# Trunk inference step on one core: cumulated gates spread by transposes of a repeated column, the fox bias added by VectorE, the decays masked ahead of the fox maxima

## The chip, the cores and the metric

The kernel runs as one program on 1 core of a Trainium2 chip. The metric is device time in microseconds (us), median of several runs; a smaller number is better. TensorE is called PE here, VectorE DVE, ScalarE ACT, GpSimd POOL, and the engine that issues all transfers SP.

## The reference, cut to what matters

Two decoder layers run over a prompt of 256 tokens and over 8 sampled tokens, each of which has 1024 past tokens. In each layer a half-step FFN is followed by four groups of heads that one projection feeds, and by a second half-step FFN. Three of the groups matter here: B, forgetting ("fox") attention, whose logits get the cumulated log gates; C, the gated delta rule; A, windowed attention with a partial rotation ("rope"). The same groups attend for the 8 sampled tokens over a paged cache.

```python
def fox_attend(q, k, v, cum_k, cum_q, q_pos):
    s = einsum('nqhd,nkhd->nhqk', q, k) * HEAD_DIM ** -0.5
    s = s + cum_q[..., :, None] - cum_k[..., None, :]
    s = where(k_pos[None, :] <= q_pos[:, None], s, -inf)
    return einsum('nhqk,nkhd->nqhd', softmax(s), v)
...
# group C, in chunks
gcum = cumsum(gch, axis=-1)
decay = exp(where(i[:, None] >= i[None, :], gcum[..., :, None] - gcum[..., None, :], -inf))
a_mat = where(strict, einsum('...id,...jd->...ij', kbeta, kc) * decay, 0.0)
t_mat = triangular_solve(eye + a_mat, eye)
```

## The kernel before, in words

Each engine has its own program, written out by hand in the order in which it runs, and waits on named semaphores. There is no scheduler. Each layer is a row of stages: gate and up products, down products, the input projection, then the mixing stage ("mix", from PE's transposes at L1714 to the output projection), the output projection and the second FFN. The dense stages run fp32 as three products of rounded parts. The change touches only the first part of mix, once in each of the two layers.

Names: `cum` holds for each token the running sums of the log gates, columns 0 to 3 and 8 to 11 for fox and 4 to 7 and 12 to 15 for the delta rule; DVE copies it out of PSUM at L1214. The rows over keys that both groups need (one value for each key, on every partition) are made by PE in two steps: four transposes to 4 partitions (L1767), copied by DVE to `rows` (L1264 to L1266, signal `rows`), then matmuls with `head_rows` that spread a row over 128 partitions: four of 384 columns into the fox scores (L1788) and eight of 128 columns for the decays (L1792, signal `gate_mm` 3). The causal mask goes into the fox scores as a matmul with the identity (L1776), so scores, mask and bias accumulate in PSUM banks 0 to 3.

From there DVE takes the fox maxima (`row_max(0)`, L1277 to L1279), then subtracts and masks the decays `dt_` (L1302, signal `dt_masked`). ACT runs the eight exponentials of `softmax(0)` and then the one of the decays (L777, signal `gate_act` 4). POOL waits for that at L947: it makes two masked copies of `dt_` (L950, L951), and only after them the products of the sampled queries with the cached keys: for each of the 8 samples four instructions of 512 columns (L988), one of 256 (L990) and one of 512 (L991). DVE sums these products in `sample_add(b)` (L1311, L1313, signal `s_red`).

SP's queue is one long list. `keys(b)` loads the keys of sample b in 11 transfers and, from sample 2 on, waits until the products of sample b-2 are summed, since the buffer is reused:

```python
def keys(b):
    i, use = b % 2, b // 2
    if use:
        sp.wait_ge(S("s_red"), V("s_red", 2 * b - 2))
        queries(b)
```

After `keys(3)` come small transfers of the state, `keys(4)`, `vals(2)`, `keys(5)`, `vals(3)`, eight stores, and so on to `vals(5)`. SP reads page numbers (L432) between them. Before all that, SP waits at L493 for both rotations (`rope` 2) before it stores the sampled queries and loads `vals(0)` and `vals(1)`.

DVE's order after the decays is: `probs_out(0)`, `attend_scale(0)` (L1295), `sample_add(0)`, the squares of the sampled convolution (L1369 to L1371, signal `mix_ss` 2), `row_max(1)` (L1281 to L1283, for group A), L1374, the delta block (L1413 to L1421, which reads the k-k products of L1879 in PSUM and POOL's masked copies), `probs_out(1)` (L1288) and `sample_add(1)`. ACT's order is: L803 (waits for `mix_ss` 2), `softmax(1)` (L766), the two copies of the turned matrix `tm` (L808), `probs_out(1)`.

## Time and profile before

| What | Value |
|---|---|
| median of 3 runs | 1450.3 us (1449.67, 1450.3, 1457.71) |
| profiled execution, its own time | 1457.6 us |
| its span | 1455.7 us |
| mean granted PE clock | 0.923 |
| PE busy | 1320.3 us (91%) |
| DVE busy | 899.1 us (62%) |
| ACT busy | 620.2 us (43%) |
| POOL busy | 229.9 us (16%) |
| chain that ended last | PE 67%, DVE 12%, issue 8%, SPq 7%, DMA 3% |

Busy time is time in which the profile has an instruction of the engine running. The chain that ended last goes back from the last instruction, at each step to what released it; "SPq" in it is time in which SP issues transfers, and "issue" is time for which the profile shows no cause. Its shares are averages over the whole program, where the dense stages are most of the time. The profiled execution is one of the longer ones: its own time lies 7.3 us above the median.

### The profile page before, as it was taken

How to read it: one execution, taken by the hardware profiler on the slowest of the kernel's cores; microseconds unless marked ns; L12 is line 12 of the kernel's file. 1: busy time of each engine (PE TensorE's matmuls, PEld its weight loads, DVE VectorE, ACT ScalarE, POOL GpSimd, SP SyncE). 2: the span in 40 equal slices, each digit the busy share in tenths (PEclk: the TensorE clock that was granted, in tenths of full speed). 3: DMA queues.
4: the chain of work that ended last, by engine and by line, in shares of the span. 5: the costliest groups of instructions: out<-in, count | busy, mean ns of one | idle time of the engine just before them, and what ended most of it. 6: DMA issues, size and time to landing. Idle time of an engine off the chain costs nothing.

```text
span 1455.7 us, 27914 instructions
## 1 busy us (share of the span) xinstructions
PE 1320.3 (91%) x9996; PEld 1219.6 (84%) x9996; DVE 899.1 (62%) x1520; ACT 620.2 (43%) x1153; POOL 229.9 (16%) x240
## 2 busy tenths in 40 slices
PE   6999999996877899999999999999977769999998
PEld 5899998985754589999989999899666528899997
DVE  3676447866766466664476664675567664776644
ACT  3655345434020364443566644543240214644443
POOL 2000002014455020000110000100165441100000
PEclk9999999997886699999999999999678767999998
DMA  7465464534476345655655645565326653455553
GB/s 233 149 198 175 135 184 154 193 96 137 127 219 199 105 132 175 190 165 158 185 171 176 190 150 168 159 196 158 92 83 180 204 157 125 137 174 183 155 174 94
DMA packets 286122, 234.17 MB, mean 161 GB/s; under 512 B 19899, under 2 KB 282019, under 8 KB 286057
## 3 DMA queue, kind: packets, MB, share of 16 engines
q1 hardware_dynamic: 286056, 233.37, 52.4%
q8 instruction: 33, 0.54, 0.2%
q14 instruction: 33, 0.26, 0.1%
HBM read 228.65 MB, written 5.37 MB: 161 GB/s over the span
## 4 chain that ended last, share of the span: by engine, by line
PE 67%; DVE 12%; issue 8%; SPq 7%; DMA 3%; ACT 2%; POOL 2%; DVEq 0%; ACTq 0%; POOLq 0%
PE ps L1574 20%; PE ps L1575 20%; PE ps L1576 20%; DVE wlo L1011 2%; SPq L461 2%; PE ps L1865 2%; SPq L469 1%; DVE nlo L1065 1%; DVE s L1311 1%; ACT whi L608 1%; DMA raw<-in_w_in_dram 1%; DVE ps L1048 1%; PE ps L1996 1%; POOL kslot L988 1%; PE ps L1946 0%
## 5 line engine op out<-in xcount | busy, mean ns | idle before, releaser
L1574 PE MATMUL ps<-nhi,whi 128*128 128x264 f32 x1936 | 559.8, 289 | 20.0 <-DVE wlo L1011 11.6
L1575 PE MATMUL ps<-nlo,whi 128*128 128x264 f32 x1936 | 552.3, 285 | 0.0
L1576 PE MATMUL ps<-nhi,wlo 128*128 128x264 f32 x1936 | 551.8, 285 | 0.0
L1011 DVE TENSOR_TENSOR wlo<-raw,whi 128x1024 fp32r<-128x1024 f32 (+2 forms) x364 | 380.5, 1087 | 268.8 <-ACT whi L608 268.3
L608 ACT ACTIVATE whi<-raw 128x1024 fp32r<-128x1024 f32 (+2 forms) x364 | 324.9, 942 | 167.3 <-PE ps L1576 107.5
L1574 PEld LDWEIGHTS ps<-nhi,whi 128*128 128x128 f32 x1936 | 368.4, 190 | 29.5 <-DVE nlo L1065 14.7
L1575 PEld LDWEIGHTS ps<-nlo,whi 128*128 128x128 f32 x1936 | 368.8, 191 | 0.2
L1576 PEld LDWEIGHTS ps<-nhi,wlo 128*128 128x128 f32 x1936 | 366.8, 189 | 0.0
L1574 PE MATMUL ps<-hhi,whi 128*128 128x264 f32 x704 | 203.1, 288 | 9.1 <-DVE hlo L1033 9.1
L1576 PE MATMUL ps<-hhi,wlo 128*128 128x264 f32 x704 | 202.2, 287 | 0.0
L1575 PE MATMUL ps<-hlo,whi 128*128 128x264 f32 x704 | 201.8, 287 | 0.0
L1574 PEld LDWEIGHTS ps<-hhi,whi 128*128 128x128 f32 x704 | 134.6, 191 | 9.9 <-issue 9.8
L1576 PEld LDWEIGHTS ps<-hhi,wlo 128*128 128x128 f32 x704 | 134.8, 192 | 0.0
L1575 PEld LDWEIGHTS ps<-hlo,whi 128*128 128x128 f32 x704 | 134.8, 191 | 0.0
L905 POOL TENSOR_TENSOR ss_acc<-sq 128x264 f32<-128x264 f32 x12 | 9.1, 756 | 720.4 <-ACT sq L638 666.3
L628 ACT ACTIVATE hhi<-h_t 128x264 f32 (+1 forms) x88 | 37.4, 425 | 164.0 <-DVE h_t L1030 164.0
L988 POOL TENSOR_TENSOR kslot<-kslot,q_bc 128x512 f32<-128x512 f32 x64 | 79.5, 1276 | 78.4 <-DMA kslot<-in_state_swa_k_dram 78.4
L909 POOL TENSOR_TENSOR ss_acc<-ss_acc,sq 128x264 f32<-128x264 f32 x66 | 56.9, 862 | 187.3 <-ACT sq L638 165.6
L800 ACT ACTIVATE s<-s 128x104 f32<-128x104 f32 x8 | 2.3, 290 | 172.4 <-DVE s L1344 172.4
L1033 DVE TENSOR_TENSOR hlo<-h_t,hhi 128x264 f32 (+1 forms) x88 | 38.1, 433 | 59.9 <-ACT hhi L628 59.9
L623 ACT ACTIVATE s_t<-s_t 128x264 f32<-128x264 f32 x88 | 35.7, 424 | 58.2 <-DVE s_t L1023 58.1
L1023 DVE TENSOR_TENSOR s_t<-ps,ptr 128x264 f32<-128x264 f32 x88 | 36.1, 427 | 30.5 <-ACT ptr L671 21.4
(349 smaller groups left out, 1493.5 us busy)
## 6 DMA issues: line engine op xcount, KB each, us to landing
raw<-in_ffn_gate_dram SPq DMA_DIRECT2D x44, 1024.0 KB, 5.3
raw<-in_ffn_up_dram SPq DMA_DIRECT2D x44, 1024.0 KB, 5.3
raw<-in_ffn_down_dram SPq DMA_DIRECT2D x64, 704.0 KB, 4.5
raw<-in_w_in_dram SPq DMA_DIRECT2D x24, 1024.0 KB, 5.7
kslot<-in_cache_fox_k_dram SPq DMA_DIRECT2D x128, 128.0 KB, 2.8
vslot<-in_cache_fox_v_dram SPq DMA_DIRECT2D x128, 128.0 KB, 2.6
raw<-in_w_out_dram SPq DMA_DIRECT2D x8, 1024.0 KB, 5.1
kslot<-in_state_swa_k_dram SPq DMA_DIRECT2D x32, 128.0 KB, 2.8
```

The lines of the kernel that those rows point to most:

```text
L461: sp.dma_start(kslot[:, i, g, :], io["cache_fox_k"][bass.ds(page_of[b, g], 1), l].rearrange("o p h d -> p (o h d)")).then_inc(S(f"k_in{i}" ...
L608: act.activation(whi[s][:, a:b], raw[s][:, a:b], ACT.Copy).then_inc(S(f"w_hi{s}"), 1)
L623: act.activation(s_t[:, f, :], s_t[:, f, :], ACT.Silu).then_inc(S("silu"), 1)
L628: act.activation(hhi[:, bass.ds(2 * j + f, 1), :].rearrange("p o n -> p (o n)"), h_t[:, f, :], ACT.Copy).then_inc(S("h_hi"), 1)
L909: ins = tt_(ss_acc[:, :], ss_acc[:, :], sq8[:, t, :], ALU.add)
L988: ins = tt_(kslot[:, i, g:g + 2, :], kslot[:, i, g:g + 2, :], q_bc[:, i, GW:512].unsqueeze(1).broadcast_to([P, 2, GW]), ALU.mult)
L1011: tt2(wlo[s][:, a:b], raw[s][:, a:b], whi[s][:, a:b].bitcast(F32), ALU.subtract).then_inc(S(f"w_lo{s}"), 1)
L1023: tt2(s_t[:, f, :], ps[:, f, 0:N], r_pre, ALU.mult).then_inc(S("gate_taken"), 1)
L1033: tt2(hlo[:, at, :].rearrange("p o n -> p (o n)"), h_t[:, f, :], hhi[:, at, :].rearrange("p o n -> p (o n)").bitcast(F32), ALU.subtract).t ...
L1574: mm(out, wh, hi_, start=first, stop=False)
L1575: mm(out, wh, lo_, start=False, stop=False)
L1576: return mm(out, wl, hi_, start=False, stop=last)
```

## The change

It does seven things, in both layers.

1. The four transposes to `rows` and the twelve matmuls that spread the rows are gone. In their place PE transposes each of the 16 columns of `cum`, repeated 128 times by its access pattern, with the identity: a transpose of 128 equal columns gives the row on all 128 partitions. The decays come first (`gate_mm` 2), the fox rows second (`gate_mm` 3, banks 7 and 3). `rows` and its copies are gone.
2. The mask matmuls (L1776) are gone. DVE forms `fox_add` = -8 x row + mask in SBUF, three instructions of 512 columns (signal `fox_bias`), and `row_max(0)` begins with one addition of 1536 columns that writes scores plus bias to `smx`; the maxima and `softmax(0)` read it from there.
3. PE's fox scores of heads 0 to 2 stand ahead of the decayed gates of the cache (L1759 to L1764 before), those of head 3 behind them and behind a wait for `fox_bias`, since bank 3 is lent to a fox row.
4. DVE copies `cum` and masks the decays ahead of `row_max(0)`; ACT takes their exponential ahead of `softmax(0)`.
5. The rotation of the sampled tokens comes first; SP waits for it alone (`rope` 1), and for the prompt's rotation only ahead of the stores. The prompt's rotation and the products of the sampled queries with their own keys move behind `row_max(0)`. ACT's `probs_out(0)` now waits for the prompt's rotation (they share a buffer).
6. On DVE the delta block and `row_max(1)` stand ahead of `sample_add(0)`; on PE the k-k products (`kk_mm`) stand ahead of group A's scores.
7. On ACT the copies of `tm` stand ahead of `softmax(1)`; the wait for `mix_ss` 2 stands ahead of both.

```diff
@@ SP
-                    sp.wait_ge(S("rope"), V("rope", 2))
+                    sp.wait_ge(S("rope"), V("rope", 1))
                     sp.dma_start(d_q[:, 0:GW], smp[:, QA:QA + GW]).then_inc(S("q_pre"), 16)
...
                     read_pages(7)
+                    sp.wait_ge(S("rope"), V("rope", 2))
@@ ACT
-                                act.activation(smx[:, h, sl], (smx if m else ps)[:, h, sl], ACT.Exp, scale=1.0 if m else HD ** -0.5, bias=small[:, 32 + 4 * t + h:33 + 4 * t + h],
+                                act.activation(smx[:, h, sl], smx[:, h, sl], ACT.Exp, scale=1.0 if m else HD ** -0.5, bias=small[:, 32 + 4 * t + h:33 + 4 * t + h],
...
+                        if m == 0:
+                            act.wait_ge(S("rope"), V("rope", 2))
...
-                    softmax(0)
                     act.wait_ge(S("dt_masked"), V("dt_masked", 1))
                     act.activation(dt_[:, :, :], dt_[:, :, :], ACT.Exp).then_inc(S("gate_act"), 1)
+                    softmax(0)
...
-                    softmax(1)
                     act.wait_ge(S("tt_turned"), V("tt_turned", 2))
                     for t in range(NT):
                         act.activation(tm[:, t, :], ps[:, 4 + t, :], ACT.Copy).then_inc(S("tm_act"), 1)
+                    softmax(1)
@@ DVE
...
+                    dve.wait_ge(S("gate_mm"), V("gate_mm", 2))
+                    for t in range(NT):
+                        for h in range(H):
+                            ins = stt(dt_[:, t, h * P:(h + 1) * P], ps[:, 4 + t, h * P:(h + 1) * P], cum[:, 8 * t + 4 + h:8 * t + 5 + h], C("causal"), ALU.subtract, ALU.add)
+                    ins.then_inc(S("dt_masked"), 1)
+
+                    dve.wait_ge(S("gate_mm"), V("gate_mm", 3))
+                    for t, bk in ((0, 7), (1, 3)):
+                        f_row = ps[:, bk, :].rearrange("p (h n) -> p h n", h=H)
+                        for c in ((0, 1), (2,))[t]:
+                            ins = stt(fox_add[:, :, c * P:(c + 1) * P], f_row, -8.0, C("fox_mask")[:, c * P:(c + 1) * P].unsqueeze(1).broadcast_to([P, H, P]), ALU.mult, ALU.add)
+                    ins.then_inc(S("fox_bias"), 1)
...
+                        if m == 0:
+                            ch(tt2(smx, ps[:, 0:4, 0:384], fox_add[:, :, :], ALU.add))
+                            red(small[:, 32:36], smx[:, :, 0:P], AX.X, ALU.max, negate=True)
+                            ch(red(small[:, 36:40], smx[:, :, P:3 * P], AX.X, ALU.max, negate=True))
...
-                    fr = ps[0:4, 7, 0:256]
-                    gr = ps[0:4, 7, 256:512]
-                    ts(rows[:, 0:P], fr[:, 0:P], -8.0, None, ALU.mult)
-                    ts(rows[:, P:3 * P], fr, -8.0, None, ALU.mult)
-                    ts(rows[:, 3 * P:5 * P], gr, 1.0, None, ALU.mult).then_inc(S("rows"), 1)
...
                     attend_scale(0, 256)
+                    delta_front()
+                    row_max(1)
                     sample_add(0)
...
-                    row_max(1)
@@ PE
+                    for t in range(NT):
+                        for h in range(H):
+                            ins = tr(ps[:, 4 + t, h * P:(h + 1) * P], cum[:, 8 * t + 4 + h:8 * t + 5 + h].broadcast_to([P, P]), ident)
+                    ins.then_inc(S("gate_mm"), 1)
+                    for t in range(NT):
+                        for h in range(H):
+                            ins = tr(ps[:, (7, 3)[t], h * P:(h + 1) * P], cum[:, 8 * t + h:8 * t + 1 + h].broadcast_to([P, P]), ident)
+                    ins.then_inc(S("gate_mm"), 1)
...
+                    scores(*fox, range(3))
...
-                    for k, c0 in enumerate((0, 8, 4, 12)):
-                        ins = tr(ps[0:4, 7, k * P:(k + 1) * P], cum[:, c0:c0 + 4], ident)
...
-                                mm(ps[:, h, 0:3 * P], ident, C("fox_mask"), start=True, stop=False)
...
-                        ins = mm(ps[:, h, 0:3 * P], hr(h), rows[:, 0:3 * P], start=False, stop=True)
...
-                            ins = mm(ps[:, 4 + t, h * P:(h + 1) * P], hr(h), rows[:, (3 + t) * P:(4 + t) * P], start=True, stop=True)
...
+                    pe.wait_ge(S("fox_bias"), V("fox_bias", 1))
+                    scores(*fox, (3,)).then_inc(S("scores"), 1)
...
-                    pe.wait_ge(S("o_att"), V("o_att", 1))
-                    scores(1, lambda a: qkT[:, a, :], lambda a: qkT[:, 2 + a, :]).then_inc(S("scores"), 1)
                     pe.wait_ge(S("kq_act"), V("kq_act", 2))
...
+                    pe.wait_ge(S("o_att"), V("o_att", 1))
+                    scores(lambda a: qkT[:, a, :], lambda a: qkT[:, 2 + a, :]).then_inc(S("scores"), 1)
```

DVE, from the end of the products of the sampled queries with their own keys to the masks of the decays, before (`small`, `smp`, `proj` and `tok` are SBUF tiles, `ps` is PSUM, `const` holds masks and tables):

```order
L1260 TENSOR_SCALAR small<-small 8x8 [waits dve_ch]
L1264 TENSOR_SCALAR rows<-ps 4x128 [waits gate_mm,dve_ch]
L1265 TENSOR_SCALAR rows<-ps 4x256
L1266 TENSOR_SCALAR rows<-ps 4x256
L1268 COPY bias<-ps 128x8x32 [waits dec_mm]
L1269 COPY bias<-const 128x8x12
L1271 TENSOR_TENSOR kd<-proj,eg 128x512 [waits gate_act]
L1277 TENSOR_REDUCE small<-ps 128x4 [waits scores]
L1278 TENSOR_REDUCE small<-ps 128x4
L1279 TENSOR_SCALAR small<-small 128x8 [waits dve_ch]
L1302 SCALAR_TENSOR_TENSOR dt__79<-ps,cum,const 128x128 [waits gate_mm]
```

and now, from the masks of the decays to the start of the prompt's rotation:

```order
L1261 SCALAR_TENSOR_TENSOR dt__78<-ps,cum,const 128x128 [waits gate_mm]
L1261 SCALAR_TENSOR_TENSOR dt__78<-ps,cum,const 128x128 x7
L1268 SCALAR_TENSOR_TENSOR fox_add<-ps,const 128x4x128 [waits gate_mm]
L1268 SCALAR_TENSOR_TENSOR fox_add<-ps,const 128x4x128 x2
L1274 TENSOR_TENSOR proj<-ps,fox_add 128x1536 [waits scores]
L1275 TENSOR_REDUCE small<-proj 128x4 [waits dve_ch]
L1276 TENSOR_REDUCE small<-proj 128x4
L1277 TENSOR_SCALAR small<-small 128x8 [waits dve_ch]
L1298 COPY bias<-ps 128x8x32 [waits dec_mm]
L1299 COPY bias<-const 128x8x12
L1301 TENSOR_TENSOR kd<-proj,eg 128x512 [waits gate_act]
L1206 TENSOR_TENSOR ptr<-tok,const 128x64
```

The masks of the decays stood behind the maxima and now stand first; the prompt's rotation (L1206 and on, twelve instructions, then five for the own keys and five for `sx` and `v_own`) stood ahead of this piece and now stands behind it.

DVE, from the scaling of the fox output to the delta block, before:

```order
L1295 TENSOR_TENSOR otok<-ps,small 128x2x256 [waits o_mm,dve_ch]
L1311 TENSOR_REDUCE s_116<-kslot 128x32 [waits prod]
L1313 TENSOR_REDUCE s_116<-kslot 128x12 [waits prod]
L1369 MEMSET small 32x1 [waits s_silu]
L1370 TENSOR_TENSOR cv<-cv 64x64
L1371 TENSOR_REDUCE small<-cv 64x1 [waits dve_ch]
L1281 SCALAR_TENSOR_TENSOR proj<-ps,const 128x1536 [waits scores]
L1282 TENSOR_REDUCE small<-proj 128x4 [waits dve_ch]
L1283 TENSOR_REDUCE small<-proj 128x4
L1374 TENSOR_SCALAR cv<-cv,small,const 96x64 [waits mix_r]
L1413 TENSOR_TENSOR tt<-ps,ys 128x2x2x64 [waits kk_mm,dts]
```

and now:

```order
L1293 TENSOR_TENSOR otok<-ps,small 128x2x256 [waits o_mm,dve_ch]
L1370 TENSOR_TENSOR tt<-ps,ys 128x2x2x64 [waits kk_mm,dts]
L1370 TENSOR_TENSOR tt<-ps,ys 128x2x2x64 [waits kk_mm]
L1375 TENSOR_TENSOR tt<-const,tt 128x512 [waits dve_ch]
L1377 TENSOR_TENSOR at__81<-ps,at__81 128x2x2x128
L1378 TENSOR_TENSOR qkt<-ps,dt__78 128x2x2x128
L1377 TENSOR_TENSOR at__81<-ps,at__81 128x2x2x128
L1378 TENSOR_TENSOR qkt<-ps,dt__78 128x2x2x128
L1279 SCALAR_TENSOR_TENSOR proj<-ps,const 128x1536 [waits scores]
L1280 TENSOR_REDUCE small<-proj 128x4 [waits dve_ch]
L1281 TENSOR_REDUCE small<-proj 128x4
L1317 TENSOR_REDUCE s_115<-kslot 128x32 [waits prod]
```

The delta block and the maxima of group A now stand ahead of the two sums of sample 0 (`s_116<-kslot` before, `s_115<-kslot` now), and these ahead of the square that ACT waits for.

PE, from the last product for the cache's gates (L1764) on, before:

```order
L1764 MATMUL ps<-otok,const 128x256 [waits lf_sb]
L1767 MATMUL ps<-const,cum 4x128 [waits cum_sb]
L1767 MATMUL ps<-const,cum 4x128 x3
L1776 MATMUL ps<-const 128x384 [waits tok_dve,tok_act]
L1778 MATMUL ps<-proj 128x128
L1778 MATMUL ps<-proj 128x256
L1776 MATMUL ps<-const 128x384
L1778 MATMUL ps<-proj 128x128
L1778 MATMUL ps<-proj 128x256
L1776 MATMUL ps<-const 128x384
```

and now, behind the small matmuls that cumulate the gates (L1766), up to the first product for the cache:

```order
L1766 MATMUL ps<-gate,const 128x4
L1773 MATMUL ps<-const,cum 128x128 [waits cum_sb,tok_dve,tok_act]
L1773 MATMUL ps<-const,cum 128x128 x7
L1777 MATMUL ps<-const,cum 128x128 x8
L1786 MATMUL ps<-proj 128x128
L1786 MATMUL ps<-proj 128x256
L1786 MATMUL ps<-proj 128x128
L1786 MATMUL ps<-proj 128x256
L1786 MATMUL ps<-proj 128x128
L1786 MATMUL ps<-proj 128x256
L1794 MATMUL ps<-ptr,const 128x256 [waits lf_sb]
```

The sixteen transposes that spread the columns and the scores of three heads, which stood behind the products for the cache, now stand ahead of them, and the mask matmuls L1776 between the heads are gone.

## Rows read from the trace of the kernel before

**Rows 1.** Chain that ended last, layer 0's mix: start us, us, what.

```profile
308.90 2.85 PE ps L1714 x24
...
346.86 4.92 POOL kslot L988 x4
351.80 2.29 DVE s L1311
...
355.07 1.14 DVE cv L1370
356.45 1.68 DVE proj L1281
...
358.75 1.21 DVE small L1283
...
360.53 0.67 DVE tt L1413 x2
...
363.26 1.94 PE ps L1888 x8
...
366.54 0.69 DVE ptr L1288
...
370.31 0.35 SPq L473
...
444.97 1.49 SPq L452
```

**Rows 2.** The same chain, start of layer 1's mix.

```profile
1013.22 2.85 PE ps L1714 x24
```

**Rows 3.** SP's timeline, the issue that opens `keys(3)` in layer 1.

```profile
1085.16 0.34 SPq L473 DMA_DIRECT2D q_bc<-d_q  x1
```

**Rows 4.** Windows, layer 1: us, busy of PE, PEld, DVE, ACT, POOL, then clock, DMA, GB/s.

```profile
1030.00:1036.00 6.00, 6.00 (x17) 3.30 (x17) 5.66 (x29) 0.42 (x2) 0.00 (x0) 0.50 0.03 11
```

**Rows 5.** DVE's timeline, layer 0: start us, us, line, operation, tiles [idle before].

```profile
322.34 0.36 DVE L1200 TENSOR_SCALAR small<-small 128x4 f32<-128x4 f32 x2
...
330.70 0.28 DVE L1264 TENSOR_SCALAR rows<-ps 4x128 f32<-4x128 f32 x1
...
331.57 0.40 DVE L1268 COPY bias<-ps 128x256 f32<-128x256 f32 x1
...
332.02 0.67 DVE L1271 TENSOR_TENSOR kd<-proj,eg 128x512 f32<-128x512 f32 x1
...
339.55 2.16 DVE L1302 SCALAR_TENSOR_TENSOR dt__79<-ps,cum,const 128x128 f32<-128x128 f32 x8 [1.39 <-PE ps L1792]
341.62 0.18 DVE L1355 COPY sx<-const 128x64 f32<-128x64 f32 x1
...
343.34 0.69 DVE L1362 COPY proj<-ps 128x512 f32<-128x512 f32 x1 [0.65 <-PE ps L1805]
```

**Rows 6.** PE's timeline, layer 0: group A's scores and the k-k products.

```profile
350.26 1.66 PE L1778 MATMUL ps<-proj 64*128 64x128 f32 x16 [0.94 <-DVE otok L1295]
351.65 2.00 PE L1879 MATMUL ps<-proj 64*128 64x256 f32 x16
```

**Rows 7.** Line L777 (exponential of the decays): who waited for it (us, times).

```profile
  POOL ys L950: 55.2, 2
```

**Rows 8.** POOL's timeline, the products of one sample.

```profile
431.33 4.95 POOL L988 TENSOR_TENSOR kslot<-kslot,q_bc 128x512 f32<-128x512 f32 x4 [6.73 <-DMA kslot<-in_state_swa_k_dram]
```

**Rows 9.** DVE's timeline in the same stretch.

```profile
432.59 1.25 DVE L1324 SCALAR_TENSOR_TENSOR s<-s,bias 128x24 f32<-128x24 f32 x1
...
433.84 1.23 DVE L1327 COPY s<-sx 128x8 f32<-128x8 f32 x1
```

**Rows 10.** ACT's timeline, layer 0: first and last of `softmax(1)`'s sixteen, copies of `tm`.

```profile
360.00 0.40 ACT L766 ACTIVATE proj<-proj,small 128x128 f32<-128x128 f32 x1 [2.98 <-DVE small L1283]
...
363.42 0.19 ACT L766 ACTIVATION_READ_ACCUMULATOR proj<-proj,small 128x1 f32 x1
365.24 1.09 ACT L808 ACTIVATE tm<-ps 128x512 f32<-128x512 f32 x2 [1.63 <-PE ps L1888]
```

More of the change, by code:

```diff
@@ L190, in build @@
         eg = place("eg", [P, 3, 8])
-        rows = place("rows", [4, 5 * P])
         og = place("og", [P, D])
@@ L279, in build @@
         v_own = scratch("v_own", 2 * (GW + 1), [B, 2, GW + 1])
+        fox_add = place("fox_add", [P, H, 3 * P], at=state_at)
         ps = ctx.enter_context(nc.psum_tensor("ps", [P, 8, 512], F32))
@@ L1256, in _ @@
-                    own = v_own[:, 0, 0:GW]
-                    for k, (qc, kc) in enumerate(((QB_, KB_), (QA, KA))):
-                        ch(tt2(own, smp[:, qc:qc + GW], smp[:, kc:kc + GW], ALU.mult))
-                        ch(red(small[0:B, 112 + 4 * k:116 + 4 * k], own.rearrange("p (h d) -> p h d", h=H), AX.X, ALU.add))
-                    ch(ts(small[0:B, 112:120], small[0:B, 112:120], HD ** -0.5, None, ALU.mult))
-                    dve.wait_ge(S("gate_mm"), V("gate_mm", 2))
-                    fr = ps[0:4, 7, 0:256]
```

147 lines of the change are left out of this document (69 added, 78 removed).

## The prediction

> **What bounds the kernel now.** I first read the chain that ended last through mix of layer 0. Mix starts at 308.90 [rows 1]. At 370.31 the chain goes over to SP with the transfers of `keys(3)`, and at 444.97 it is still on SP, which issues one transfer after another [rows 1]. So in that layer the rest of mix starts when `keys(3)` starts, and `keys(3)` starts when `sample_add(1)` has ended on DVE (366.54 to 370.31, the copy of L1288 ahead of it) [rows 1]. The question for this change is therefore: **when does `sample_add(1)` end?** In layer 0 it is 370.31 - 308.90 = 61.4 after the start of mix. In layer 1 mix starts at 1013.22 [rows 2] and `keys(3)` at 1085.16 [rows 3], 71.9 after it: 10.5 later for the same instructions. The window that shows the difference has PE at a granted clock of 0.50, the lower level of 1.2 GHz, in 1030 to 1036, busy all the time [rows 4].
>
> **The change, part by part.** I add it up in layer 0's times, in two parts that meet at the copy L1362 (343.34 [rows 5]).
>
> *Part 1, up to that copy, DVE alone.* DVE works in one list, so the order inside it doesn't change the sum. From 322.34 to 330.70 it does the norms, `cum`, both rotations and the own products (8.4) [rows 5]. The three copies to `rows` (330.70 to 331.57) go. The cache's bias and `kd` take 331.57 to 332.69 (1.1), the decays' masks 2.2, and `sx` with `v_own` 341.62 to 342.69 (1.1) [rows 5]. New are three additions of 512 columns for `fox_add`: 0.65 each by L1288 with as many columns (0.69, the next one starts a little sooner) [rows 1], 2.0. `row_max(0)` becomes what `row_max(1)` is, 356.45 to 359.96, 3.5, and 0.3 for its scaling [rows 1]. Two waits stand in it: `cum` is now wanted before PE has cumulated the gates, about 0.6, and behind `fox_add` head 3's four matmul instructions, 0.9 by a quarter of L1778's sixteen (1.66) and a start [rows 6], 1.7 at the lower clock. Sum: 322.3 + 8.4 + 1.1 + 2.2 + 1.1 + 2.0 + 3.8 + 0.6 + 0.9 = 342.4. That is 0.9 before the 343.34 of now. PE's sixteen transposes and the removed mask and row matmuls cost or bring nothing more here, since DVE is what is late: L1888 shows eight transposes in 1.94 at worst [rows 1], so sixteen take 4, beside DVE's norms.
>
> But one thing moves that the sum doesn't hold. POOL waited 55.2 us in two waits for the exponential of the decays [rows 7]. Now the decays are masked at 322.3 + 3.4 + 1.0 + 0.6 + 2.2 = 329.5, their exponential (1.06) ends at 330.8, POOL's masked copies take about 4 more, and the products of samples 0 and 1 start at 334.8 instead of 346.86 [rows 1]. Four of 512 columns take 4.92 [rows 1], one sample has 2816 columns, so 6.8, and both 13.5. So POOL runs from 334.8 to 348 or later, and DVE comes to `kd`, the prompt's rotation, the own products and `sx` at 336.6. Before, POOL was idle beside all of these.
>
> What that does is seen at 431.33, where POOL has products of 1.24 each [rows 8]. DVE's L1324, an operation of 24 columns with both inputs in SBUF, lasts 1.25, and L1327, a copy of 8 columns from SBUF to SBUF, 1.23: each until a product of POOL has ended [rows 9]. **21 instructions of that kind** stand in the new list between the cache's bias and the copy: one copy, `kd`, twelve of the rotation, two own products and a scaling, four of `sx` and `v_own` (three copies). POOL has about 11 instructions left at 336.6. If each lets one of DVE's pass, POOL ends at 348.3 plus DVE's own 2, so 350.4, and DVE then has ten instructions and two sums left, 3.5: 353.9. I take **353.3**, 10.9 over the free sum, since L1326 (not in the rows, between the two) is so short that one may slip by now and then. The ends are 342.4 (none held) and 354.5.
>
> The Trainium skill, page SBUF — State Buffer (sections on the two separate sides and on who interferes with whom), says that a DVE instruction with two SBUF inputs and a GpSimd instruction that reads SBUF exclude one another for a whole instruction, and so do copies in a two-port mode, but not instructions fed by PSUM. By that rule all 21 are held and part 1 ends at 354; by shared bandwidth it would end near 342.4. The two rows above agree with the rule.
>
> *Part 2, from the copy to `keys(3)`.* Before: 370.31 - 343.34 = 27.0. Now: to the scaled fox output 343.34 to 350.26, 6.9 (PE's transposes, ACT's and DVE's copies, values) [rows 5, 6]. The k-k products follow the values at once, 2.00 [rows 6], of which 0.9 is covered by the scaling: 1.1. The delta block after the second of them: 3.5, from 360.53 to the L1888 that its first half releases at 363.26, and two more of 0.6 [rows 1]. `row_max(1)` 3.5, `sample_add(0)` 351.80 to 355.07, 3.2, the square and its sum 0.4 now that POOL is idle beside it (355.07 to 356.45 before, 1.14 for the square) [rows 1]. Then **a wait that the change adds**: ACT's L803 waits for that sum, and behind it in ACT's list are the copies of `tm` and all of `softmax(1)`; before, `softmax(1)` ran beside DVE's delta block. So on the path: two small ACT operations 0.5, `tm` 1.1, `softmax(1)` 360.00 to 363.61, 3.6 [rows 10], PE's first eight transposes 1.5, and L1288 with `sample_add(1)` 3.8 [rows 1]. Sum: 6.9 + 1.1 + 3.5 + 3.5 + 3.2 + 0.4 + 0.5 + 1.1 + 3.6 + 1.5 + 3.8 = 29.1. PE has been idle ahead of the copy and ahead of the second transposes; at the lower level its terms (transposes, values, k-k) cost up to 3.4 more. I take **30**, 3 more than now.
>
> Together `keys(3)` comes at 353.3 + 30 = 383.3, **13.0 later** in layer 0. Almost all of it is DVE's, so layer 1 gets the same 74.4 after its start where it had 71.9: **2.5 later**, since the 10.5 that it lost to the low clock is mostly PE work that is removed or now covered. 1457.6 + 13.0 + 2.5 = **1473**.
>
> What is free: `rope` 1 lets SP load `vals(0)` and `vals(1)` some 4 us sooner, and nothing waits for them; SP then stands at `keys(2)`, whose sample_add(0) comes about 17 later than at 351.80, but `keys(3)` waits longer still. The later wait for `rope` 2 on SP is long fulfilled. ACT's new wait for `rope` 2 holds `probs_out(0)`, which PE wants only behind its own transposes. The shift is carried to the end, since SP has no wait from `keys(3)` to `vals(5)` to absorb it.
>
> **The profiled execution and the median.** The median lies 7.3 below. An execution in which layer 1 has less of the low clock would be shorter by about that. The new kernel hardly depends on that stretch, so I compare with the longer one and keep 1473; if the difference has another cause, the result is 7 lower.
>
> **Rivals.** *A, nothing is held.* DVE's small instructions slip in beside POOL (for: DVE's and POOL's are both short of a full load; against: 1.25 and 1.23 [rows 9]). Then `keys(3)` is at 342.4 + 30 = 372.4: +2.1 in layer 0, -8.4 in layer 1, 1451. This is the case that is not slower, by one mechanism: the removed PE work at the low clock of layer 1. It decides when the hold is under 2 us per layer. *B, two pass for each of POOL's.* Half the hold: -5 per layer, 1463. *C, more behind it.* POOL's products of sample 2 now fall on `sample_bias(0)` (L1323 to L1327), which gates the levels of the triangular inverse, and PE is at the low level there: +3 per layer, 1479. *D, the early decays don't come early* because the exponential or PE's rows are late by several us: POOL then starts beside part 2 instead, with fewer instructions to hold, 1458.
>
> **How the numbers follow.** Forecast 0.45, A 0.17, B 0.2, C 0.13, D 0.05. A measurement of this kernel can tell about 1%, 14.5 us: the bounds are 1436 and 1465. Slower: nearly all of the forecast and C and half of B, 0.66. Faster needs A with part 2 as short as before and the 7 us of the median besides, 0.03. Same: 0.31. The range goes from 1456, where the forecast and B end if the median's 7 us have another cause, to 1481, which is C with PE at the low level throughout; A below 1456 and part of D are left out.
>
> **What would show it.** Right: POOL's first product 26 us after the start of mix instead of 38; the twelve instructions of the prompt's rotation with durations near 1.2 instead of 0.22, and the copy of L1362 about 44 after the start; `keys(3)` about 74 after it in both layers; `softmax(1)` behind the square. Wrong: rotation durations of 0.22 beside POOL's products, or SP waiting after `keys(3)` for something else, so that the shift isn't carried.

## The result

The changed kernel takes 1474.9 us (median of 4 runs, 1473.7 to 1478.5) against 1450.0 before (median of 4, 1443.2 to 1457.7): a ratio of 1.0174, 95% interval 1.0121 to 1.0228. It is slower. Ratios here and below leave out executions of a second, slower state of the chip, such as one of the twelve with the products late (1642.2 us at a granted clock of 0.75). Its profiled execution took 1474.8, 17.2 more than the profiled one of before.

Page of the profile after: its span, the busy time of the engines, and the shares of the chain that ended last.

```profile
span 1472.8 us, 27836 instructions
...
PE 1295.2 (88%) x9956; PEld 1207.0 (82%) x9956; DVE 913.0 (62%) x1522; ACT 620.2 (42%) x1153; POOL 232.9 (16%) x240
...
PE 67%; DVE 14%; SPq 9%; issue 4%; ACT 3%; DMA 2%; DVEq 0%; ACTq 0%; POOL 0%; POOLq 0%
```

DVE now holds 14% of the chain where it held 12%, and PE's busy time is 25 us less than before: work was removed, and the time went up.

Chain that ended last in mix of layer 0, after: start us, us, what. It answers to [rows 1].

```profile
308.36 2.84 PE ps L1725 x24
...
340.09 1.23 DVE ptr L1207
...
370.08 2.19 DVE s L1317
...
374.29 0.96 ACT tm L811 x2
375.25 3.51 ACT proj L768 x16
...
380.81 0.69 DVE ptr L1286
```

Start of mix in layer 1 by the same chain:

```profile
1026.63 2.84 PE ps L1725 x24
```

SP's timeline after, the issues that open `keys(3)` in layer 0 and in layer 1 (they answer to the SP rows of [rows 1] and [rows 3]):

```profile
384.58 0.35 SPq L474 DMA_DIRECT2D q_bc<-d_q  x1
...
1103.14 0.34 SPq L474 DMA_DIRECT2D q_bc<-d_q  x1
```

Read together: mix starts at 308.36, the copy of L1387 starts at 351.8, `keys(3)` at 384.58, which is 43.4 and 76.2 after the start. In layer 1 `keys(3)` comes 1103.14 - 1026.63 = 76.5 after it. Before it was 61.4 and 71.9. So `keys(3)` is 14.8 and 4.6 later. The first product of the output projection, the end of mix, follows: 192.5 after the start instead of 178.0 in layer 0, 194.3 instead of 190.5 in layer 1. These are 14.6 and 3.8 more, and the span differs by 17.1.

Timeline of DVE and POOL after, layer 0, in the order of starts (other engines' rows left out):

```profile
333.92 4.95 POOL L992 TENSOR_TENSOR kslot<-kslot,q_bc 128x512 f32<-128x512 f32 x4
334.06 1.21 DVE L1276 TENSOR_REDUCE small<-proj 128x4 f32<-128x1024 f32 x1
335.31 1.14 DVE L1277 TENSOR_SCALAR small<-small 128x8 f32<-128x8 f32 x1
...
336.36 0.41 DVE L1298 COPY bias<-ps 128x256 f32<-128x256 f32 x1
...
337.64 1.79 DVE L1301 TENSOR_TENSOR kd<-proj,eg 128x512 f32<-128x512 f32 x1
...
338.82 1.19 POOL L994 TENSOR_TENSOR kslot<-kslot,q_bc 128x256 f32<-128x256 f32 x1
...
341.20 4.92 POOL L992 TENSOR_TENSOR kslot<-kslot,q_bc 128x512 f32<-128x512 f32 x4
341.24 1.30 DVE L1208 TENSOR_TENSOR ptr<-tok,const 128x64 f32<-128x64 f32 x1
...
346.08 0.72 POOL L994 TENSOR_TENSOR kslot<-kslot,q_bc 128x256 f32<-128x256 f32 x1
...
346.80 1.29 DVE L1207 TENSOR_TENSOR ptr<-tok,const 128x64 f32<-128x64 f32 x1
348.02 0.21 DVE L1208 TENSOR_TENSOR ptr<-tok,const 128x64 f32<-128x64 f32 x1
...
351.77 0.67 DVE L1387 COPY proj<-ps 128x512 f32<-128x512 f32 x1
```

Here is the mechanism. From L1277 (335.31) to the second L1207 (346.80) DVE runs twelve instructions. L1298, which is fed by PSUM, is not held. Each of the other eleven is held until an instruction of POOL's ends, one for each that POOL had left: the scaling L1277, the copy L1299 (1.01), `kd`, and eight of the prompt's rotation (1.18 to 1.31 beside products of 512 columns, 0.74 and 0.65 beside the two of 256). Ten of them end within 0.1 us behind POOL's instruction; `kd`, the largest, ends 0.6 behind it, and POOL's next one waits for that. An operation of 64 columns takes 1.3 beside POOL; the same one takes 0.21 at 348.02, as POOL's last instruction ends. The same happens to POOL: its L994 of 256 columns takes 1.19 beside `kd` and 0.72 at 346.08.

A window of the profile after (us, busy of PE, PEld, DVE, ACT, POOL, then PE's clock, DMA share, GB/s):

```profile
345.00:360.00 15.00, 7.41 (x34) 7.30 (x36) 8.81 (x22) 6.46 (x10) 3.02 (x3) 0.52 0.00 1
```

PE's timeline after, the transposes that follow the copy and the k-k products:

```profile
352.59 1.94 PE L1840 MATMUL ps<-const,tok 128*128 128x128 f32 x8 [9.99 <-DVE proj L1387]
...
359.47 3.50 PE L1885 MATMUL ps<-proj 64*128 64x256 f32 x16
```

PE had no work for 10 us ahead of L1840, and after it the granted clock is near its lower level, 1.2 GHz: 0.52 of full speed between 345 and 360, and the k-k products take 3.50 where they took 2.00 [rows 6]. In the scores of group A, from 362.8 on, it is back at 1.00.

### The profile page after: what moved, and what is told of

The parts are those of the page before. It is cut to its first block, busy times and chain, and to the rows that moved or that the text cites. A ratio compares the mean times of both kernels' runs of the same rounds, so it can differ in the third digit from the quotient of the medians.

```text
span 1472.8 us, 27836 instructions
## 1 busy us (share of the span) xinstructions
PE 1295.2 (88%) x9956; PEld 1207.0 (82%) x9956; DVE 913.0 (62%) x1522; ACT 620.2 (42%) x1153; POOL 232.9 (16%) x240
## 4 chain that ended last, share of the span: by engine, by line
PE 67%; DVE 14%; SPq 9%; issue 4%; ACT 3%; DMA 2%; DVEq 0%; ACTq 0%; POOL 0%; POOLq 0%
PE ps L1585 20%; PE ps L1586 19%; PE ps L1587 19%; DVE wlo L1015 2%; SPq L462 2%; SPq L470 2%; PE ps L1873 1%; DVE nlo L1069 1%; ACT whi L610 1%; DVE s L1317 1%; DMA raw<-in_w_in_dram 1%; DVE ps L1052 1%; SPq L433 1%; PE ps L2005 1%; PE ps L1725 1%
## 5 line engine op out<-in xcount | busy, mean ns | idle before, releaser
L1037 DVE TENSOR_TENSOR hlo<-h_t,hhi 128x264 f32 (+1 forms) x88 | 38.2, 434 | 59.9 <-ACT hhi L630 59.9
```

The source lines that it names most:

```text
L1037: tt2(hlo[:, at, :].rearrange("p o n -> p (o n)"), h_t[:, f, :], hhi[:, at, :].rearrange("p o n -> p (o n)").bitcast(F32), ALU.subtract).t ...
```

## The experiments

All runs are timed against the kernel before on the same chip; a ratio stands with its 95% interval. "After" is the changed kernel. The table has, from the profile of each, the start of the copy of L1387 (L1362 in the kernel before), of `keys(3)` and of the output projection, in us from the start of mix, layer 0 / layer 1, and the span.

| Kernel | copy | keys(3) | end of mix | span | median, ratio to before |
|---|---|---|---|---|---|
| before | 34.4 / 44.6 | 61.4 / 71.9 | 178.0 / 190.5 | 1455.7 | |
| before, second profile | 34.8 / 34.8 | 62.2 / 62.2 | 181.0 / 181.4 | 1450.7 | one run, 1452.6 |
| after | 43.4 / 43.4 | 76.2 / 76.5 | 192.5 / 194.3 | 1472.8 | 1474.9, 1.0174 |
| products late | 33.8 / 33.2 | 62.4 / 61.8 | 180.6 / 180.6 | 1443.3 | 1447.8, 0.9971 |
| exponential late | 38.4 / 38.4 | 71.3 / 71.2 | 190.8 / 187.1 | 1462.8 | 1467.2, 1.0112 |
| ACT's wait behind | 43.4 / 43.4 | 74.0 / 74.4 | 191.9 / 196.9 | 1468.9 | 1473.6, 1.0152 |
| both (1st and 3rd) | 33.2 / 33.9 | 59.6 / 60.4 | 176.5 / 177.0 | 1435.7 | 1438.4, 0.9930 |
| PE kept busy | 43.5 / 43.5 | 71.5 / 74.8 | 191.7 / 194.1 | 1472.2 | 1473.0, 1.0126 |
| both, first sum first | 33.4 / 33.2 | 59.4 / 59.2 | 178.1 / 176.7 | 1440.9 | 1441.8, 0.9920 |
| rotation back | 36.5 / 36.5 | 66.5 / 66.7 | 187.0 / 187.7 | 1459.4 | 1457.2, 1.0037 |
| both sums early | 33.2 / 33.2 | 55.2 / 55.1 | 180.6 / 181.2 | 1446.2 | 1446.0, 0.9955 |
| before, second sum early | 34.3 / 44.7 | 58.3 / 68.7 | 178.0 / 186.9 | 1452.0 | 1448.0, 0.9975 |
| products halved | 43.0 / 42.3 | 75.4 / 74.8 | 194.3 / 194.3 | 1471.8 | 1474.6, 1.0160 |
| both, third products late | 33.5 / 33.2 | 59.9 / 59.7 | 177.7 / 182.7 | 1444.4 | 1443.6, 0.9961 |

### Products late

```diff
@@ POOL, in the loop over the samples, ahead of its products
+                        if b == 0:
+                            pool.wait_ge(S("kq_dve"), V("kq_dve", 1))
```

> The changed kernel, but POOL waits for DVE's copy L1387 before the products of sample 0; its masked copies of the decays stay where they are. My theory (a DVE instruction with both inputs in SBUF is held until a POOL instruction ends): the prompt's rotation takes 0.15 to 0.42 an instruction instead of 1.2, the copy comes about 34 us after the start of mix instead of 43.5, keys(3) about 67 instead of 76.2 and 76.5, 9.5 less in each layer: 1456. Rival (the rotation is slow for a reason of its own, such as its strided operands or DMA traffic): durations and time as in the changed kernel, 1475. Rival (the hold moves to the instructions behind the copy, so that part of it comes back): 1460 to 1466.

Measured: 1447.8, ratio 0.9971 (0.9942 to 0.9999), so 27 less than after, where 19 were expected. DVE's rows of that profile (line numbers are 2 higher):

```profile
334.70 0.17 DVE L1279 TENSOR_SCALAR small<-small 128x8 f32<-128x8 f32 x1
...
335.23 0.68 DVE L1303 TENSOR_TENSOR kd<-proj,eg 128x512 f32<-128x512 f32 x1
...
335.84 0.21 DVE L1208 TENSOR_TENSOR ptr<-tok,const 128x64 f32<-128x64 f32 x1
...
340.92 0.67 DVE L1389 COPY proj<-ps 128x512 f32<-128x512 f32 x1
...
341.67 4.95 POOL L994 TENSOR_TENSOR kslot<-kslot,q_bc 128x512 f32<-128x512 f32 x4 [8.93 <-DVE proj L1389]
```

The maxima's scaling is down from 1.14 to 0.17, `kd` from 1.79 to 0.68, the rotation from 1.3 to 0.21; POOL's products start behind the copy. The copy comes 9.6 and 10.2 earlier, as the theory of the hold says; that the rotation is slow by itself is ruled out. But `keys(3)` is 13.8 and 14.7 earlier. From the copy to `keys(3)` it is now 28.6 instead of 32.8 (layer 0), and that difference is PE's; its pieces save 4.8, and 0.5 goes back, since DVE's L1377 (1.23 instead of 0.69) now stands beside POOL's products. The same window in this profile:

```profile
345.00:360.00 15.00, 4.83 (x44) 3.94 (x43) 12.49 (x17) 6.26 (x11) 10.81 (x10) 0.78 0.04 10
```

PE's timeline, the same two rows:

```profile
341.74 1.06 PE L1842 MATMUL ps<-const,tok 128*128 128x128 f32 x8 [1.04 <-DVE proj L1389]
...
345.36 2.00 PE L1887 MATMUL ps<-proj 64*128 64x256 f32 x16
```

The wait for the copy is 1.04 instead of 9.99, the clock in 345 to 360 is 0.78 instead of 0.52, the eight transposes take 1.06 instead of 1.94, and the k-k products 2.00 (in layer 1 also). So the hold cost 10 on DVE and then 4 more through PE's clock, in each layer.

### Exponential late

```diff
@@ ACT
+                    softmax(0)
                     act.wait_ge(S("dt_masked"), V("dt_masked", 1))
                     act.activation(dt_[:, :, :], dt_[:, :, :], ACT.Exp).then_inc(S("gate_act"), 1)
-                    softmax(0)
```

> The changed kernel, but ACT takes the exponential of the decays behind softmax(0), as before the change. Nothing of DVE's or PE's order differs. My theory: POOL's masked copies start about 33 us after the start of mix and the products about 37, when DVE has all but a few of the small instructions behind it; the copy L1387 at 34 to 37 us, keys(3) at 67 to 70: 1456 to 1462. So the early exponential alone would hold most of the loss. Rival (the moved rotation costs what it costs wherever POOL is): 1475. Rival (the delta block now waits for POOL's masked copies): about 1465.

Measured: 1467.2, 1.0112 (1.0083 to 1.0141). The copy comes at 38.4, a little behind what was expected, and 8 us of the loss are given back, not 13 or more. The timeline of DVE and POOL shows what was missed:

```profile
338.57 1.65 POOL L954 TENSOR_TENSOR ys<-dt__78,const 128x256 f32<-128x256 f32 x2 [20.40 <-ACT dt__78 L781]
...
340.17 2.34 POOL L955 TENSOR_TENSOR at__81<-dt__78,const 128x1024 f32<-128x1024 f32 x1
340.30 2.29 DVE L1381 TENSOR_TENSOR sx<-sx,small 8x64 f32<-8x64 f32 x1
```

The rotation is past when POOL starts, but five instructions of the own keys, `sx` and `v_own` are not, and one of POOL's masked copies is its longest instruction: L955 (2.34) holds L1381, an addition on 8 partitions, for 2.29. The price of being held is the length of what POOL runs at that time. PE was idle for 6.13 ahead of its transposes in this kernel, and its k-k products took 3.58: the part that goes by the clock was lost in full.

### Rotation back

The rotation of the prompt, the own products, `sx` and `v_own` (22 instructions) stand ahead of the masks of the decays again; nothing else differs from after.

```diff
@@ DVE
+                    rope(tok[:, :, 0:512]..., P, 2, C("cos"), C("sin"), w4)
+                    ... (own products, sx, v_own)
                     dve.wait_ge(S("gate_mm"), V("gate_mm", 2))
                     for t in range(NT):
```

> The changed kernel with the prompt's rotation, the own products, sx and v_own back ahead of the masks of the decays, where they stood before the change; the early decays and everything else stay. POOL's products then start about 31 us after the start of mix instead of 25.6, and only the scaling of the maxima, the cache's bias and kd meet them. My theory (the loss is the number of instructions that stand beside POOL): 3 to 4 held instead of 12, copy at 36 to 38 us, keys(3) at 65 to 70: 1452 to 1461. Rival (the early start of POOL costs the same whatever stands beside it): 1475. Rival (the later decays and maxima cost what the order saves): 1463 to 1468.

Measured: 1457.2, 1.0037 (1.0010 to 1.0064), copy at 36.5, `keys(3)` at 66.5 and 66.7: as the first theory said. So the early decays by themselves cost little; the loss came from what the same change had put beside POOL's products. PE goes on to its transposes without a wait here, and its k-k products take 2.00 in both layers.

### Products halved

```diff
@@ POOL
-                        for g in range(0, NPG, 2):
-                            ins = tt_(kslot[:, i, g:g + 2, :], ..., q_bc[:, i, GW:512]..., ALU.mult)
+                        for g in range(NPG):
+                            ins = tt_(kslot[:, i, g, :], kslot[:, i, g, :], q_bc[:, i, GW:512], ALU.mult)
```

> The changed kernel with each POOL product of 512 columns for the fox pages split in two of 256. Theory (a DVE instruction is held until the POOL instruction that runs has ended, and one passes for each): the rotation's instructions take 0.6 to 0.7 us instead of 1.2 beside these, and more of them pass, but POOL has more instructions too, so its last one ends as late; the copy L1387 at 41 to 44 us after the start of mix and the time 1470 to 1475. Rival (the rotation's instructions are slowed by shared bandwidth): their durations stay at 1.2 with the smaller products.

Measured: 1474.6, 1.0160 (1.0105 to 1.0215). Timeline of DVE and POOL:

```profile
333.95 5.97 POOL L992 TENSOR_TENSOR kslot<-kslot,q_bc 128x256 f32<-128x256 f32 x8
...
339.93 0.76 DVE L1208 TENSOR_TENSOR ptr<-tok,const 128x64 f32<-128x64 f32 x1
...
340.57 1.27 POOL L995 TENSOR_TENSOR kslot<-kslot,q_bc 128x512 f32<-128x512 f32 x1
340.62 1.31 DVE L1209 TENSOR_TENSOR ptr<-tok,const 128x64 f32<-128x64 f32 x1
...
342.53 0.76 DVE L1211 TENSOR_TENSOR tok<-ptr 128x64 f32<-128x64 f32 x1
```

Beside products of 256 columns the rotation takes 0.76, beside the one of 512 columns (L995) 1.31, and 0.76 again. A shared bandwidth would not step with the size of the neighbour's instruction. Seventeen instructions are held instead of eleven, most for about half as long, and the copy comes within 1.2 of where it came.

### PE kept busy

```diff
@@ PE
                     turn_p(0)
+                    for k in range(72):
+                        tr(ps[:, 5, (k % 4) * P:(k % 4 + 1) * P], ident, ident)
                     pe.wait_ge(S("rope"), V("rope", 2))
```

> The changed kernel with 72 more transposes of the identity on PE, in a bank that nobody reads then, in the 10 us in which it waits for the prompt's rotation. DVE's hold stays as it is. My theory (the hold costs twice: once on DVE, and once because PE, idle for 10 us, comes back at the lower clock): the copy L1387 stays at 43.4 us after the start of mix, the k-k products take 2.0 instead of 3.5, and from the copy to keys(3) it is 28.6 as with the products late instead of 32.8: 4.2 less in each layer, 1466.5. Rival (the lower clock comes from something other than that idle time): k-k products 3.5 and 1475. Rival (the filler runs on past the rotation and delays PE): 1475 to 1480.

Measured: 1473.0, 1.0126 (1.0083 to 1.0169). Windows of this profile:

```profile
345.00:360.00 15.00, 12.13 (x111) 11.24 (x109) 11.28 (x27) 7.36 (x11) 2.97 (x3) 1.00 0.01 2
...
428.00:448.00 20.00, 16.58 (x119) 12.59 (x111) 13.68 (x30) 3.72 (x26) 7.78 (x6) 0.81 0.69 212
...
468.00:488.00 20.00, 12.40 (x79) 5.22 (x77) 10.93 (x28) 2.44 (x5) 5.86 (x7) 0.66 0.70 217
```

PE's timeline, the k-k products:

```profile
356.17 2.00 PE L1887 MATMUL ps<-proj 64*128 64x256 f32 x16
```

In layer 0 the clock is 1.00 in 345 to 360, the k-k products take 2.00, and `keys(3)` is 4.7 earlier with the copy where it was: in this layer the clock's share of the loss is real, and it follows from PE's idle time. In layer 1 it is only 1.7. There PE still waited 2.96 for the copy behind the added transposes (2.45 in layer 0); its eight transposes took 1.06, at the higher level, but in the products that follow the clock fell while PE was working, and the k-k products took 3.38. So the idle time is not all that decides. And the end of mix comes just 0.9 and 0.2 earlier, so the forecast of 1466.5 failed. In layer 0, whose mix starts at nearly the same time in both profiles, the clock later on was 0.81 and 0.66 (428 to 448, 468 to 488), against these windows in the profile of after:

```profile
428.00:448.00 20.00, 15.52 (x126) 10.79 (x127) 12.98 (x23) 7.57 (x60) 7.96 (x8) 0.91 0.67 199
...
468.00:488.00 20.00, 12.37 (x85) 5.52 (x85) 12.45 (x29) 0.69 (x3) 10.07 (x9) 0.76 0.65 201
```

Part of the gain was lost to a lower clock further on. PE's products with the cached values that SP waits for behind `vals(5)` start 4.3 earlier (459.85 instead of 464.14), but take 8.6 instead of 6.8, and SP goes on 2.5 earlier. The last such products start 2.6 earlier (483.46 instead of 486.02) and take 8.7 instead of 6.2. Whether the added transposes caused the lower clock, or whether it lies within what single executions differ by, these runs don't settle.

### ACT's wait behind, alone and together with the products late

```diff
@@ ACT
-                    act.wait_ge(S("mix_ss"), V("mix_ss", 2))
-                    ... (its two operations)
                     act.wait_ge(S("tt_turned"), V("tt_turned", 2))
                     ... (copies of tm)
                     softmax(1)
+                    act.wait_ge(S("mix_ss"), V("mix_ss", 2))
+                    ... (its two operations)
```

> The changed kernel, but ACT's wait for the sum of squares (mix_ss 2) and its two operations stand behind the copies of tm and softmax(1). My theory (keys(3) sets the end, and softmax(1) stands behind sample_add(0) only by that wait): softmax(1) starts as row_max(1) ends, 61.7 us after the start of mix instead of 66.8, keys(3) at 71 instead of 76.2: 5.2 less in each layer, 1464.5. Rival (the end is carried by something that the wait does not move, such as the levels of the triangular inverse): 1473 to 1475. Rival (DVE's scaling of the sampled convolution, which waits for ACT, now comes late and takes the gain back): 1470.

> The edits of the first and the third of these together. My theory, if both savings are on the one path that ends in keys(3): 14.7 less in each layer, keys(3) at 61.5 us after the start of mix in both layers, which is where layer 0 had it before the change and 10.4 earlier than layer 1 had it: 1445.5, a little faster than before the change (1450.0). Rival (another chain, the inverse's levels or the products of POOL, is late next): 1450 to 1456. Rival (PE stays longer at the lower clock as it idles more): up to 3 more a layer, 1451.

Measured: alone 1473.6, 1.0152 (1.0125 to 1.0179); together 1438.4, 0.9930 (0.9899 to 0.9961). Alone it moved `keys(3)` by 2.2, not 5.2. DVE's timeline (ACT's wait behind alone, layer 0) has the second sum of `sample_add(1)`:

```profile
377.92 0.94 DVE L1319 TENSOR_REDUCE s<-kslot 128x12 f32<-128x768 f32 x1
```

SP's timeline of the same kernel has the starts of `keys(2)`, of the store `d_cn` and of `keys(3)`:

```profile
372.49 0.33 SPq L474 DMA_DIRECT2D q_bc<-d_q  x1
...
381.10 0.58 SPq L517 DMA_DIRECT2D d_cn<-cv  x1
381.73 0.43 SPq L474 DMA_DIRECT2D q_bc<-d_q  x1
```

`sample_add(1)` ends at 378.9 (377.92 + 0.94), but SP comes to `keys(3)` only at 381.73. From the start of `keys(2)`, 372.49, SP issues twelve transfers (the queries and the eleven of the keys), the four of `gb` and the one of `d_cn` without a pause: 9.2. So `keys(3)` can't start less than 9.2 behind `keys(2)`, which starts when `sample_add(0)` ends. None of the three forecasts for this run had it. Together, the two edits bring `keys(3)` to 59.6 and 60.4 where 61.5 was expected: the first gives 13.8 and 14.7 instead of 9.5, the second on top of it 2.8 and 1.4 instead of 5.2. That kernel is 0.7% faster than the one before the change, the best that these runs found but for one that ties with it.

### Further along the same chain

Four kernels looked for what is late next. The first two:

```diff
@@ DVE (on top of both)
                     attend_scale(0, 256)
+                    sample_add(0)
                     delta_front()
                     row_max(1)
-                    sample_add(0)
@@ DVE (on top of products late and the edit above, with ACT's order tm, wait, softmax(1))
                     ts(cv[:, 8, :], ...).then_inc(S("s_conv"), 1)
+                    sample_add(1)
                     ...
                     probs_out(1)
-                    sample_add(1)
```

> The kernel with both edits, and sample_add(0) ahead of the delta block and row_max(1), as before the change. Theory (the end is set by keys(3), which follows keys(2) by the 9.2 us that SP needs for what lies between them, and keys(2) follows sample_add(0)): keys(2) 44 us after the start of mix instead of 50.4, keys(3) 53 to 54 instead of 59.6, 6 less in each layer, 1426. Rival (the chain of the inverse's levels on PE and DVE is nearly as late, and the delta block now comes 3 later): 1438 to 1444, no gain. In between if SP's saving counts only until the levels bind: 1434.

> The kernel with the products late and sample_add(0) first, and now sample_add(1) as well ahead of probs_out(1): DVE's list is sample_add(0), delta block, row_max(1), the square, the scaling, sample_add(1), probs_out(1). On ACT the copies of tm stand first, then the wait for the square, then softmax(1). Theory (in the kernel with the first sum alone moved, keys(3) at 59.4 waited for sample_add(1), which stood behind softmax(1) and PE's transposes): sample_add(1) ends at 54.5 us after the start of mix, keys(3) there too, 5 less in each layer, 1432. Rival (the inverse's levels set the end from here on): keys(3) at 54.5 but the end of mix 118 or more behind it no longer holds, and the time stays at 1438 to 1442.

Measured: 1441.8, 0.9920 (0.9891 to 0.9948), and 1446.0, 0.9955 (0.9929 to 0.9982). The first shows no gain over both edits alone (0.9930); the second looks a little slower than the first, but their intervals overlap. In the first `keys(2)` starts at 42 and still `keys(3)` at 59: my forecast of 53 forgot that `sample_add(1)` stands behind `softmax(1)` and PE's transposes. In the second `keys(3)` starts at 55, 4 earlier, and mix ends 2.5 and 4.5 later than in the first. DVE's timeline of the second, layer 0, with the same hold in a new place:

```profile
370.21 0.69 DVE L1295 TENSOR_TENSOR otok<-ps,small 128x512 f32<-128x512 f32 x1 [6.19 <-PE ps L1834]
370.81 1.16 DVE L1331 SCALAR_TENSOR_TENSOR s<-s,bias 128x64 f32<-128x64 f32 x1
...
373.15 1.23 DVE L1335 COPY s<-sx 128x8 f32<-128x8 f32 x1
```

DVE copies the probabilities of group A behind `sample_add(1)`, so PE's values come later (6.19 of waiting), and POOL's products of sample 3 lie on `sample_bias(0)`: its six instructions, 370.81 to 374.8, take 4.0 where they took 0.9 in the kernel before the change. This was rival C's mechanism; in the changed kernel itself it stayed away, but the kernel with both edits had it too (3.5). With that the levels of the inverse are late, and `sample_add(2)` among them: `keys(4)` waits for it until 82.2 and 80.4. So in this kernel `keys(3)`, at 55, no longer sets the end.

```diff
@@ POOL (on top of both)
+                        if b == 2:
+                            pool.wait_ge(S("s_max"), V("s_max", 1))
```

> The kernel with both edits (products late, ACT's wait behind), and POOL waits once more: its products of sample 2 start only when DVE has ended sample_bias(0) (signal s_max 1), whose six instructions POOL's products stretched from about 0.9 to 3.3 us. Theory (the same hold, at a second place on the chain of DVE and PE that comes next after keys(3)): the six take 0.9, 2.4 less ahead of the inverse's levels, and sample_add(2), which comes some 10 us after POOL's products of sample 2, does not notice them 3 us later: between 0 and 2.4 less in each layer, 1434 to 1438. Rival (the products of sample 3, which follow, now meet more of DVE's instructions and give it back): 1438 to 1441.

Measured: 1443.6, 0.9961 (0.9938 to 0.9984), no better than the 0.9930 of both edits. The six instructions took 0.9 as expected instead of 3.5, and `sample_add(2)` came at 73.4 instead of 75.5, but in layer 0 `keys(4)` stayed at 79.7 against 79.5: SP was issuing until then. Nobody waited there for what was saved. In layer 1 `keys(4)` came at 81.1 instead of 80.3 and mix ended 5.7 later (182.7); neither forecast had that, and its cause stays open.

```diff
@@ DVE (the kernel before)
+                    sample_add(1)
                     probs_out(1)
-                    sample_add(1)
```

> The kernel before the change, with sample_add(1) ahead of the copy of probs_out(1) instead of behind it; nothing else. Theory (keys(3) sets the end in both kernels): sample_add(1) follows the delta block, which ends at about 55, so keys(3) comes at 58 to 59 us after the start of mix instead of 62, 3 less in each layer, 1444. Rival (the end of mix is tied to DVE's and PE's levels, and these lose 3 by it): 1450 to 1453.

Measured: 1448.0, 0.9975 (0.9936 to 1.0015). `keys(3)` came at 58.3 instead of 61.4 to 62.2, as expected, but a gain is not shown. The profile says where it went in layer 0, whose mix ended at 178.0 as before: PE's products with the cached values that SP waits for behind `vals(5)` started 3.0 earlier than in the first profile of before (445.89 instead of 448.90), but took 8.9 instead of 6.0, at a granted clock of 0.51 instead of 0.80, so SP went on at the same time. In layer 1 mix ended 3.6 earlier.

### The kernel before once more

> The kernel before, once more with a profile. My working took the profiled execution of 1457.6 as the one to compare with, since layer 1's mix was 12.5 longer than layer 0's in it at a granted clock of 0.50. If that stretch is what varies, this profile has another share of the low clock in one of the layers, and the time goes with it: 1450 with less of it, 1457 with as much. Rival: the executions differ elsewhere and the mix of layer 1 takes the same 190.5 us as in the first profile whatever the time is.

Measured: 1452.6, span 1450.7. Windows of layer 1 in this profile:

```profile
1028.00:1040.00 12.00, 10.68 (x62) 7.33 (x60) 11.48 (x43) 2.77 (x11) 1.21 (x3) 1.00 0.01 3
```

Mix starts at 1017.84 here, so this is 10 to 22 us after its start, and the clock is 1.00; in the first profile it was 0.50 in 1030 to 1036, 17 to 23 us after the start [rows 4]. The copy stands at 34.8 in layer 1 instead of 44.6, and mix of layer 1 takes 181.4 instead of 190.5, mix of layer 0 3.1 more. So the stretch at the low clock varies between executions of the same kernel. The profile of the kernel with only its second sum early, which is the same up to that place, has it again (copy at 44.7 in layer 1). That it is what the first profile had above the median is not shown: this one, without it, still lies 2.7 above the median of the runs beside it (1450.0).

## Why the prediction was right

**The size.** 1473 was forecast, 1474.9 measured, inside the range of 1456 to 1481.

**Part 1, the hold.** Forecast: POOL's first product 26 after the start, rotation near 1.2, copy 44.4 after the start (353.3), about 11 instructions held. Measured: 25.6; 1.2 to 1.3 for six of the rotation's twelve, 0.7 for two beside the shorter products and 0.2 for the last four; 43.4; eleven. One of the eleven is the scaling of the maxima, which the prediction had at 0.3 and did not count among its 21; it took 1.14. I had let POOL end at 350.4, since DVE's instructions would pass between; POOL's end was 348.0, so they cost it little, except for `kd`. The free sum of 342.4, or 33.5 after the start, was tested by the kernel with the products late: 33.8, which is 0.6 ahead of the first profile of before (0.9 was forecast against that one) and 1.0 ahead of the second; so little is all that the removed work brings where the clock is high. That kernel gives rival A's case by an edit, and at 1447.8 it lies near that rival's 1451. Rival B (two pass for each of POOL's) is ruled out by the eleven. Rival D fell with POOL's start. Rival C's place was free: `sample_bias(0)` began at 388.41, as POOL's products of sample 2 ended.

**Part 2, from the copy to `keys(3)`.** Forecast 30, measured 384.58 - 351.8 = 32.8. By the terms: the scaled output 8.5 for 6.9, the k-k products 2.7 for 1.1, the second transposes 2.0 for 1.5, and the others within 0.3. All three are PE's. The prediction said that the lower clock could cost up to 3.4 more and took 0.9 of it. The first two came behind the 10 us that PE waited for the rotation, with the clock near 0.5 until 362.8. The third has nothing to do with the hold: in 362.8 to 366.7 the clock was back at 1.00, and the second transposes came behind another 12.2 us without work; with the products late, all twelve at this place took 2.82, as in the changed kernel. The mechanism stood in the text, but not the link from the hold to PE's idle time, which makes most of it a consequence rather than a chance. This is the term that was too small, by 2.8 and 3.1.

**ACT's new wait** is where it was expected, `softmax(1)` starts at 375.25 behind `tm`. What it costs was overrated: in the full sum it stands with 5.2, but with it gone `keys(3)` gains 2.2, since SP's issues from `keys(2)` on are next. Only when the rest is faster too do both count: the two edits alone give 27.1 and 1.3, together 36.5.

**The shift to the end.** +13.0 and +2.5 were forecast for `keys(3)`, +14.8 and +4.6 came. Of the 19.4, 18.4 arrived at the ends of mix. In the table the end of mix lies 116 to 123 behind `keys(3)` while `keys(3)` itself runs from 58 to 76: it carries the end there, with 3 us of scatter to either side. At 55 it doesn't (125 and 126). For a shift as small as that scatter the rule is not shown: in layer 0, 4.7 gained with PE kept busy and 3.1 with the second sum early arrived as 0.9 and nothing. The prediction saw no wait of SP's from `keys(3)` to `vals(5)`; behind `vals(5)` there is one, for PE, and that is where these two gains were lost or reduced.

**The median.** The sum came to +15.5 and the two profiled executions differ by 17.2, but the medians by 24.9. I had kept the longer execution as the base, because the new kernel hardly has the stretch that varies. Both profiles of before bear this out: in the second, without that stretch, `keys(3)` stands at 62.2 in both layers, 14.0 and 14.3 ahead of after, and mix ends 11.5 and 12.9 earlier than after. These are 24.4 together, close to the 24.9 of the medians, and the forecast of 74.4 for `keys(3)` gives 12.2 twice against 62.2. So against an execution without the stretch the change costs some 24, not 15.5. The runs agree in that the kernel before lay between 1440.9 and 1461.6 here and after between 1473.7 and 1478.5, though after has only four. From the median as a base the same sum would have given 1466; that 1473 came so near rests on the choice of base as much as on the terms.

## What to carry to other kernels

When a change starts POOL's work earlier, list what DVE does beside it: each DVE operation with two SBUF inputs, and each copy or scaling from SBUF to SBUF, waited here for the end of one POOL instruction, however small it was, so many tiny ones are the worst thing to put there, and one wait on POOL's side takes the loss back. Then follow the engine that waits for them: here the clock was at its lower level behind PE's idle time, and the loss was nearly half as large again (4.2 and 4.5 on top of 9.6 and 10.2). And before a term is booked, look for what is late next: the 9.2 us that SP needs between two loads made a saving of 5.2 worth 2.2.

## What the runs showed of the hardware

- Where both had work, DVE and POOL alternated one for one: eleven of DVE's by eleven of POOL's in the changed kernel. Held were operations with two SBUF inputs, copies from SBUF to SBUF and scalings in SBUF, down to 8 columns or 8 partitions; not held were reductions (L1276, 1.21 beside POOL, and 1.21 with the exponential late, where POOL is idle then) and operations that read PSUM (L1298, 0.41 and 0.42). An exception: the copy L1334 of 8 columns took 0.16 between two held ones, in layer 0 with both edits and with both sums early. The Trainium skill, page SBUF — State Buffer, section "SBUF: two separate sides", describes an exclusive lock of the pair of ports for the whole instruction; the traces agree, by 1.31, 0.76 and 0.21 us for one operation beside products of 512, of 256 columns and beside nothing.
- POOL is held as well: 1.19 instead of 0.72 for a product beside `kd`.
- The same stretch of the kernel before ran at a granted clock of 0.50 in one execution and 1.00 in another, and mix of that layer differed by 9.0 us.
